# Thirty-two more empty columns in front of the split activations of a three-block transformer kernel

## Chip, core and metric

The kernel runs on one core of a Trainium2 chip. Its time is the device time of one execution in microseconds, of which the median over several executions counts; lower is better.

## What is computed

The reference chains three transformer blocks over one sequence of 512 tokens with 1024 channels, all in float32. Every dense layer is a product of the normed activations with a large weight matrix, and the feed-forward layers have an inner width of 2816.

```python
def reference(x, c, w_ada, ...):
    x = first_block(x, c, ...)     # ffn, spatial gating + forgetting attention, ffn
    x = second_block(x, ...)       # ffn, rwkv7 recurrence + convolution, ffn
    return third_block(x, ...)     # twice: sparse + differential attention, ffn

def swiglu(h, w_gate, w_up, w_down):
    return (jax.nn.silu(h @ w_gate) * (h @ w_up)) @ w_down
```

## The kernel before

The plan of the program (`whole_plan`) is a list of ten sublayers: six feed-forward layers (`ffn`) and four mixers. All large weight matrices are cut on the host into 264 units of 128 partitions by 2048 columns (1 MiB each). SyncE loads them one after the other into the two buffers of the tile `RAW` (`load`, L2093), each as soon as the unit two before it has been split.

A float32 product is computed as three products in the format fp32r. A unit is split by ScalarE into its rounded part (`WH`, L2435) and by VectorE into the rest (`WL = RAW - WH`, L2640). The activations are split in the same way: after a feed-forward boundary into `HH` and `HL`, after a mixer's boundary into `EH` and `EL` (`halves`), and the inner activations of a feed-forward layer into `AH` and `AL` (L2568, L2685). TensorE then multiplies high by high, high by low and low by high into the same PSUM bank; this is `mm3`, L2134 to L2138, and nearly all of TensorE's work goes through its three lines. Each of the matmuls is preceded by a load of its stationary operand.

`mm3` is used in two ways. In `project` (the first matmuls of a feed-forward layer and the projections of the mixers) a block of 128 columns of `WH` or `WL` is stationary, and 512 columns of `EH`, `EL`, `HH` or `HL` are moving. In `enter`, at the start of a sublayer, the same is done in halves of 256 columns, because the second half of the tokens arrives later. In `part` (the down projections, and the products that lead out of the mixers) the roles are turned: 128 tokens of `AH`, `AL`, `HH` or `HL` are stationary, and 512 columns of `WH` or `WL` are moving.

The tiles lie in SBUF in the order in which `build_program` asks for them, one behind the other, each rounded up to 32 bytes per partition. What comes ahead of the point that the change touches is, in bytes per partition, `X` (16384), `RAW`, `WH`, `WL` (16384 each), `A` (45056), `R`, `R0`, `V` (2048 each), `SG` (4096) and `ONES` (512): all multiples of 512. Then follow `PV` with 390 columns (1568 bytes after rounding), `CV` with 72 (288 bytes), `CN` with 776 (3104 bytes) and `LINE`, a tile of 8 columns (32 bytes) that nothing reads or writes. These four come to 4992 bytes, which is 9 times 512 and 384 more.

Behind `LINE` lie `E` (32768 bytes per partition), whose memory `EH` and `EL` share, and `G` (49152 bytes), whose memory `HH`, `HL`, `AH` and `AL` share, and then small tiles: `ST`, `ATT`, `IDB`, `MKC`, `MKB`, `PICK`, `FLOOR`, `W3`, `M8`, `GLU_LAST`, `LAM`, `PC2`. All split activations therefore start 384 bytes behind a multiple of 512 from the start of `X`, while `WH` and `WL` start on such a multiple.

The order of the work is set by the engines' own instruction streams and by semaphores; no address enters into it.

Of the kernel before, what the change touches and what calls it, by code (L numbers as in the profile page):

```python
# [25 lines left out]
P = 128  # L26
# [92 lines left out]
def build_program(nc, T, plan):  # L119
# [4 lines left out]
    def sb(name, shape, dt=F32):  # L124
        return ctx.enter_context(nc.sbuf_tensor(name, shape, dt))

    with ctx:
# [12 lines left out]
        PV = sb("PV", [P, T["pv"].shape[1]])  # L140
        CV = sb("CV", [P, VECTORS * KD])
        CN = sb("CN", [P, T["cn"].shape[1]])
        sb("LINE", [P, 8])
        with nc.sbuf_tensor("EH", [P, KD, S], F32R) as EH, nc.sbuf_tensor("EL", [P, KD, S], F32R) as EL:
            pass
        E = sb("E", [P, 16, S])
# [2956 lines left out]
def launch_parts(a, plan, nc):  # L3103
    arrays, cols, cncols = laid_out(a, plan)
    T = {n: nc.dram_tensor("in_" + n, x.shape, mybir.dt.from_np(x.dtype), kind="ExternalInput").ap()
         for n, x in arrays.items()}
    T["out"] = nc.dram_tensor("out_x", (S, D), F32, kind="ExternalOutput").ap()
    T["cols"], T["cncols"] = cols, cncols
    build_program(nc, T, plan)
    return {"in_" + n: x for n, x in arrays.items()}  # L3110
# [11 lines left out]
```

## Time and profile before

| | before |
|---|---|
| median of 3 runs | 3654.48 us (3650.88 to 3655.13) |
| the profiled execution | 3657.05 us |
| span of the profiled execution | 3655.3 us |
| TensorE matmul busy | 3482.2 us, 95% of the span, 19430 matmuls |
| weight loads busy | 2770.4 us, 76% |
| VectorE busy | 1837.7 us, 50% |
| ScalarE busy | 1152.5 us, 32% |
| GpSimd busy | 162.7 us, 4% |
| mean granted TensorE clock | 0.979 of 2.4 GHz |

In the names of instructions, `PS<-EH,WH` is a matmul into PSUM with `EH` as the moving and `WH` as the stationary operand; `128*128 128x512` means 128 partitions, 128 stationary columns and 512 moving columns. Both operands of a matmul of `mm3` are printed as f32. A matmul is shown from its start to the modelled end of its result, so that two neighbours overlap: what tells the pace is the distance from start to start. A window counts every instruction that overlaps it.

### The profile page before, as it was taken

How to read it: one execution, taken by the hardware profiler on the slowest of the kernel's cores; microseconds unless marked ns; L12 is line 12 of the kernel's file. 1: busy time of each engine (PE TensorE's matmuls, PEld its weight loads, DVE VectorE, ACT ScalarE, POOL GpSimd, SP SyncE). 2: the span in 40 equal slices, each digit the busy share in tenths (PEclk: the TensorE clock that was granted, in tenths of full speed). 3: DMA queues.
4: the chain of work that ended last, by engine and by line, in shares of the span. 5: the costliest groups of instructions: out<-in, count | busy, mean ns of one | idle time of the engine just before them, and what ended most of it. 6: DMA issues, size and time to landing. Idle time of an engine off the chain costs nothing.

```text
span 3655.3 us, 47516 instructions
## 1 busy us (share of the span) xinstructions
PE 3482.2 (95%) x19430; PEld 2770.4 (76%) x19436; DVE 1837.7 (50%) x2690; ACT 1152.5 (32%) x1728; POOL 162.7 (4%) x136
## 2 busy tenths in 40 slices
PE   9999899899999999998799999999999999899999
PEld 7887776678887888767588888666888886578887
DVE  6667535522334223798742225796422358952233
ACT  2222434422223222442342224335322233442222
POOL 0000000000000000000000001330000022200000
PEclk7999999999999999999999999999999999999999
DMA  6455221122222222220022222110222221112222
GB/s 245 178 182 196 81 95 47 58 81 92 92 92 88 100 94 92 81 79 15 8 87 92 96 98 94 70 69 24 81 93 100 95 93 70 47 53 92 92 93 81
DMA packets 47846, 330.29 MB, mean 90 GB/s; under 512 B 5312, under 2 KB 5568, under 8 KB 9280
## 3 DMA queue, kind: packets, MB, share of 16 engines
q1 hardware_dynamic: 41216, 290.09, 22.0%
q0 software_dynamic: 6464, 37.80, 2.8%
q8 instruction: 127, 2.08, 0.2%
q14 instruction: 39, 0.32, 0.0%
HBM read 325.77 MB, written 2.10 MB: 90 GB/s over the span
## 4 chain that ended last, share of the span: by engine, by line
PE 81%; DVE 13%; ACT 3%; issue 1%; DMA 0%; SPq 0%; DVEq 0%; ACTq 0%
PE PS L2136 24%; PE PS L2138 24%; PE PS L2137 24%; DVE WL L2640 2%; PE PS L319 1%; DVE A L1148 1%; DVE M L1147 1%; ACT WH L2435 1%; PE PS L394 1%; DVE X L2775 1%; PE PS L376 1%; PE PS L324 1%; PE PS L1493 1%; PE PS L931 1%; DVE A L2748 1%
## 5 line engine op out<-in xcount | busy, mean ns | idle before, releaser
L2640 DVE TENSOR_TENSOR WL<-RAW,WH 128x2048 fp32r<-128x2048 f32 x264 | 613.7, 2324 | 309.0 <-ACT WH L2435 308.6
L2136 PE MATMUL PS<-EH,WH 128*128 128x512 f32 (+1 forms) x1536 | 584.4, 380 | 28.9 <-DVE EL L2806 11.5
L2136 PE MATMUL PS<-HH,WH 128*128 128x512 f32 (+1 forms) x1456 | 556.0, 382 | 47.7 <-DVE HL L2806 23.4
L2137 PE MATMUL PS<-EL,WH 128*128 128x512 f32 (+1 forms) x1536 | 581.1, 378 | 0.0
L2138 PE MATMUL PS<-EH,WL 128*128 128x512 f32 (+1 forms) x1536 | 580.9, 378 | 0.0
L2435 ACT ACTIVATE WH<-RAW 128x2048 fp32r<-128x2048 f32 x264 | 503.9, 1909 | 191.6 <-PE PS L2138 183.5
L2137 PE MATMUL PS<-HL,WH 128*128 128x512 f32 (+1 forms) x1456 | 546.8, 376 | 0.0
L2138 PE MATMUL PS<-HH,WL 128*128 128x512 f32 (+1 forms) x1456 | 546.2, 375 | 0.0
L2679 DVE TENSOR_TENSOR A<-SG,PS 128x512 f32 (+1 forms) x132 | 90.7, 687 | 807.6 <-ACT SG L2565 807.6
L2565 ACT ACTIVATE SG<-PS 128x512 f32<-128x512 f32 x132 | 78.8, 597 | 1099.3 <-PE PS L2138 1099.3
L2136 PE MATMUL PS<-WH,AH 128*128 128x512 f32 x1056 | 417.7, 396 | 0.3 <-DVE CV L2868 0.3
L2138 PE MATMUL PS<-WH,AL 128*128 128x512 f32 x1056 | 417.1, 395 | 0.0
L2137 PE MATMUL PS<-WL,AH 128*128 128x512 f32 x1056 | 417.1, 395 | 0.0
L2136 PEld LDWEIGHTS PS<-HH,WH 128*128 128x128 f32 x1456 | 279.6, 192 | 114.6 <-issue 45.3
L2136 PEld LDWEIGHTS PS<-EH,WH 128*128 128x128 f32 x1536 | 291.8, 190 | 91.6 <-issue 13.6
L2138 PEld LDWEIGHTS PS<-EH,WL 128*128 128x128 f32 x1536 | 291.7, 190 | 58.6
L2137 PEld LDWEIGHTS PS<-EL,WH 128*128 128x128 f32 x1536 | 291.8, 190 | 58.4
L2138 PEld LDWEIGHTS PS<-HH,WL 128*128 128x128 f32 x1456 | 279.6, 192 | 52.2
L2137 PEld LDWEIGHTS PS<-HL,WH 128*128 128x128 f32 x1456 | 280.2, 192 | 50.5 <-issue 0.2
L2685 DVE TENSOR_TENSOR AL<-A,AH 128x1024 fp32r<-128x1024 f32 x66 | 80.3, 1224 | 368.6 <-ACT AH L2568 368.6
L2136 PEld LDWEIGHTS PS<-WH,AH 128*128 128x128 f32 x1056 | 198.4, 188 | 48.5 <-DVE CV L2868 0.4
L2138 PEld LDWEIGHTS PS<-WH,AL 128*128 128x128 f32 x1056 | 198.3, 188 | 47.8
(417 smaller groups left out, 3798.8 us busy)
## 6 DMA issues: line engine op xcount, KB each, us to landing
RAW<-in_w SPq DMA_DIRECT2D x264, 1024.0 KB, 4.8
E<-in_ada POOLq DMA_DIRECT2D x28, 1024.0 KB, 5.0
E<-in_ada SPq DMA_DIRECT2D x4, 1024.0 KB, 11.7
G<-in_ada SPq DMA_DIRECT2D x4, 1024.0 KB, 20.4
X<-in_x SPq DMA_DIRECT2D x1, 2048.0 KB, 13.9
X<-in_xn POOLq DMA_DIRECT2D x1, 2048.0 KB, 11.5
out_x<-A SPq DMA_DIRECT2D x4, 512.0 KB, 2.8
R<-in_row_ffn_post POOLq DMA_DIRECT2D x4, 256.0 KB, 3.1
```

Source lines behind the costliest of these rows:

```text
L319: nc.tensor.matmul(score_bank(x, i), pair["q"](i)[rows], pair["k"]((i + 1) * P)[rows], start=True, stop=False)
L324: last = nc.tensor.matmul(score_bank(x, i)[:, c0:c0 + right.shape[-1]], left, right, start=False, stop=a == len(added) - 1)
L376: last = nc.tensor.transpose(bank[:, c:c + P], probs(pair, g, x, i)[:, b * P:(b + 1) * P], IDENT)
L394: last = nc.tensor.matmul(PM[BANK_O][rows, b * P:S], pair["v"](x, b), PT[:, x, K_AT[b]:K_AT[b] + S - b * P], start=a == 0, stop=a == NT - 1)
L2136: nc.tensor.matmul(out, wh, xh, start=start, stop=False)
L2137: nc.tensor.matmul(out, wh, xl, start=False, stop=False)
L2138: return nc.tensor.matmul(out, wl, xh, start=False, stop=stop)
L2435: nc.scalar.activation(WH[:, w % 2, :], RAW[:, w % 2, :], ACT.Copy).then_inc(w_hi, 1)
L2565: nc.scalar.activation(SG[:, u % 2, :], PS[4 + 2 * (u % 2)][:], ACT.Silu).then_inc(silu_done, 1)
L2640: nc.vector.tensor_tensor(WL[:, w % 2, :], RAW[:, w % 2, :], WH[:, w % 2, :].bitcast(F32), ALU.subtract).then_inc(w_lo, 1)
L2679: nc.vector.tensor_tensor(A[:, bass.ds(u + i, 1), :].rearrange("p o s -> p (o s)"), SG[:, u % 2, :], PS[5 + 2 * (u % 2)][:], ALU.mult)\
L2685: nc.vector.tensor_tensor(AL[:, n % 2, :, :], A[:, bass.ds(2 * n + 2 * i, 2), :], AH[:, n % 2, :, :].bitcast(F32), ALU.subtract).then_inc( ...
```

## The change

The tile `LINE`, which holds no data, gets 40 columns instead of 8. Everything behind it in SBUF moves up by 128 bytes per partition: `E` with `EH` and `EL`, `G` with `HH`, `HL`, `AH` and `AL`, and the small tiles after them. The four tiles between `ONES` and `E` now come to 5120 bytes, ten times 512, so that the split activations start at a multiple of 512 bytes from `X`, as the split weights do. No instruction is added, removed or moved, and no wait changes.

```diff
@@ -140,7 +140,7 @@
         PV = sb("PV", [P, T["pv"].shape[1]])
         CV = sb("CV", [P, VECTORS * KD])
         CN = sb("CN", [P, T["cn"].shape[1]])
-        sb("LINE", [P, 8])
+        sb("LINE", [P, 40])
         with nc.sbuf_tensor("EH", [P, KD, S], F32R) as EH, nc.sbuf_tensor("EL", [P, KD, S], F32R) as EL:
             pass
         E = sb("E", [P, 16, S])
```

## Rows read from the trace of the kernel before

**Rows 1.** The page: busy times, TensorE's clock, and the chain that ended last.

```profile
PE 3482.2 (95%) x19430; PEld 2770.4 (76%) x19436; DVE 1837.7 (50%) x2690; ACT 1152.5 (32%) x1728; POOL 162.7 (4%) x136
...
PEclk7999999999999999999999999999999999999999
...
PE 81%; DVE 13%; ACT 3%; issue 1%; DMA 0%; SPq 0%; DVEq 0%; ACTq 0%
PE PS L2136 24%; PE PS L2138 24%; PE PS L2137 24%; DVE WL L2640 2%; PE PS L319 1%; DVE A L1148 1%; DVE M L1147 1%; ACT WH L2435 1%; PE PS L394 1%; DVE X L2775 1%; PE PS L376 1%; PE PS L324 1%; PE PS L1493 1%; PE PS L931 1%; DVE A L2748 1%
```

**Rows 2.** Groups of TensorE's matmuls by form: count, busy us, mean ns, idle before.

```profile
L2136 PE MATMUL PS<-EH,WH 128*128 128x512 f32 x1280 | 506.8, 396 | 6.8 <-DVE WL L2640 6.8
L2136 PE MATMUL PS<-HH,WH 128*128 128x512 f32 x1152 | 461.9, 401 | 11.9 <-DVE WL L2640 6.1 <-DVE HL L2658 2.9 <-DVE A L1848 1.9
L2136 PE MATMUL PS<-WH,AH 128*128 128x512 f32 x1056 | 417.7, 396 | 0.3 <-DVE CV L2868 0.3
L2136 PE MATMUL PS<-WH,HH 128*128 128x512 f32 x448 | 180.2, 402 | 9.1 <-DVE HL L2658 6.5 <-issue 1.7 <-DVE R L2651 0.9
L2136 PE MATMUL PS<-HH,WH 128*128 128x256 f32 x304 | 94.0, 309 | 35.8 <-DVE HL L2806 23.4 <-DVE HL L2803 12.5
L2136 PE MATMUL PS<-EH,WH 128*128 128x256 f32 x256 | 77.7, 303 | 22.2 <-DVE EL L2806 11.5 <-DVE EL L2803 10.7
```

**Rows 3.** Windows on TensorE: busy us (matmuls), granted clock, DMA share, GB/s.

```profile
760.00:960.00 200.00, 200.00 (x859) 1.00 0.25 89
990.00:1090.00 100.00, 100.00 (x430) 1.00 0.27 95
1140.00:1350.00 210.00, 210.00 (x901) 1.00 0.27 95
1390.00:1470.00 80.00, 80.00 (x345) 1.00 0.28 100
...
330.00:430.00 100.00, 100.00 (x432) 1.00 0.32 118
```

**Rows 4.** Timeline of 512-column matmuls with their weight loads: start, duration, instruction.

```profile
1000.23 0.40 PE L2138 MATMUL PS<-WH,AL 128*128 128x512 f32 x1
1000.23 0.19 PEld L2136 LDWEIGHTS PS<-WH,AH 128*128 128x128 f32 x1
1000.47 0.39 PE L2136 MATMUL PS<-WH,AH 128*128 128x512 f32 x1
1000.47 0.19 PEld L2137 LDWEIGHTS PS<-WL,AH 128*128 128x128 f32 x1
1000.70 0.40 PE L2137 MATMUL PS<-WL,AH 128*128 128x512 f32 x1
```

**Rows 5.** Timeline of 256-column matmuls on TensorE, 63 intervals between these two.

```profile
2969.71 0.28 PE L2138 MATMUL PS<-HH,WL 128*128 128x256 f32 x1
...
2977.19 0.28 PE L2138 MATMUL PS<-HH,WL 128*128 128x256 f32 x1
```

**Rows 6.** Groups of weight loads: 128 and 64 columns.

```profile
L2136 PEld LDWEIGHTS PS<-WH,AH 128*128 128x128 f32 x1056 | 198.4, 188 | 48.5 <-DVE CV L2868 0.4
...
L394 PEld LDWEIGHTS PS<-G,E 128*64 128x64 f32 x128 | 7.9, 136 | 11.2 <-issue 8.9 <-DVE A L509 1.9
```

**Rows 7.** Timeline of two sums over float32 tiles against `ONES`.

```profile
1767.72 3.70 PE L1630 MATMUL PS<-A,ONES 128*128 128x512 f32 x8
...
1778.76 3.70 PE L1640 MATMUL PS<-G,ONES 128*128 128x512 f32 x8 [1.14 <-ACT G L1773]
```

**Rows 8.** Groups of VectorE and ScalarE by form.

```profile
L2685 DVE TENSOR_TENSOR AL<-A,AH 128x1024 fp32r<-128x1024 f32 x66 | 80.3, 1224 | 368.6 <-ACT AH L2568 368.6
...
L1907 DVE TENSOR_TENSOR G<-G 128x512 f32<-128x512 f32 x12 | 8.2, 686 | 0.1
L1907 DVE TENSOR_TENSOR G<-A,G 128x512 f32<-128x512 f32 x12 | 8.2, 686 | 0.1
...
L2568 ACT ACTIVATE AH<-A 128x1024 fp32r x48 | 51.0, 1062 | 405.4 <-PE PS L2138 405.4
L2484 ACT ACTIVATE A<-X 128x1024 f32<-128x1024 f32 x40 | 42.5, 1064 | 82.3 <-DVE ST L2766 47.5 <-DVE X L2775 34.8
```

**Rows 9.** Groups within 900 to 950 us: the weights' split.

```profile
L2640 DVE TENSOR_TENSOR WL<-RAW,WH 128x2048 fp32r<-128x2048 f32 x5 | 11.5, 2293 | 5.1 <-ACT WH L2435 5.1
```

**Rows 10.** DMA issues: count, KB each, median us to landing.

```profile
RAW<-in_w SPq DMA_DIRECT2D x264, 1024.0 KB, 4.8
E<-in_ada POOLq DMA_DIRECT2D x28, 1024.0 KB, 5.0
```

## Prediction, made before the change was run

> **What bounds the kernel now.** I read the page first, for the shares and the chain that ended last. TensorE is busy for 95% of the span at a granted clock of nearly 1, and the chain runs over it for 81%, of which the three lines of `mm3` are 72% [rows 1]. So I went on to its matmuls by form. Each of `mm3`'s lines has the same counts: 1280 + 1152 + 1056 + 448 = 3936 matmuls of 512 columns, and 304 + 256 = 560 of 256 columns; three lines make 11808 and 1680 [rows 2]. Busy times overlap, so the pace has to come from windows without idle time and from the timeline. A window of 200 us in a feed-forward layer overlaps 859 matmuls; since each is drawn for 0.39 us and not 0.233, some 1.7 of them began before it, and 200 / 857.3 is 233.3 ns from start to start [rows 3]. The 256-column form takes (2977.19 - 2969.71) / 63 = 118.7 ns [rows 5]. In all 11808 x 0.2333 + 1680 x 0.1187 = 2755 + 199 = 2954 us, 81% of the span. The whole question is whether these two paces move; the instruction streams, waits and transfers are the same in both kernels. 1 ns on each 512-column matmul is 11.8 us, or 0.3% of the time.
>
> **Is there anything to win?** 512 columns at 2.4 GHz, the level that the granted clock of 1.00 stands for [rows 3], are 213.3 ns, and 256 are 106.7. The matmuls thus take 20.0 and 12.0 ns more than their columns. That excess, 11808 x 20.0 + 1680 x 12.0 = 256 us, is the most that any address could give back. The change can touch it only if it comes from where the operands lie. There are three ways, and the rows answer two.
>
> First, the place of the moving operand by itself. In the projections the moving operand is `EH` or `HH`, at 384 bytes past a multiple of 512, and the stationary one is `WH`, at 0. In the down products it is the other way round. The first sort stands in the windows from 760 and from 1140 us, the second in those from 990, 1390 and 330 us. By the same count, the paces are 233.3 and 233.5 ns for the first sort (200 / 857.3, 210 / 899.3), and 233.5, 233.0 and 232.4 ns for the second (100 / 428.3, 80 / 343.3, 100 / 430.3) [rows 3]. A matmul more or less at the edge of a window moves these by up to 0.7 ns, so they are one pace within 0.5%. A stream that begins at 0 is no faster than one that begins at 384, and so with the load. I book nothing for it.
>
> Second, the place of one operand against the other. Their distance modulo 512 is 384 or, with the roles turned, 128; the change makes it 0, which no fp32r matmul of this trace has. The nearest rows are float32 matmuls with the stationary `ONES`, at 0: eight with moving `A`, also at 0, and eight with moving `G`, at 384, take the same 3.70 us [rows 7]. They stream at about half the pace, so they speak for no effect but not at the full rate.
>
> Third, the overlap itself. The load of the next stationary block starts with the running matmul [rows 4]. A load of 128 columns takes 188 ns, one of 64 takes 136, so a column costs 0.81 ns and the reading of 128 some 104 ns, an estimate from these two [rows 6]. A 256-column matmul therefore has a load beside it nearly throughout; a 512-column one has the same single load and then 256 columns that run mostly alone. Those further 256 columns take 233.3 - 118.7 = 114.6 ns, against 106.7 by the clock: they are slow as well, by 7.9 ns. If clashes with the load made the excess, both widths would carry the same one, and they carry 12.0 and 20.0. Of each matmul's excess only 12.0 - 7.9 = 4.1 ns doesn't grow with the columns, and only that can be a clash with the load. Further, the load advances by 4 bytes in 0.81 ns and the stream by 4 bytes in about 0.42, so during one load the distance between their addresses runs through some 104 / 0.42 x 4 - 512 = 480 bytes, nearly a full turn of 512. Whatever clash there is at some distance is met in every load already; the start only shifts when. So I take 0 of the possible 4.1 ns, and keep 4.1 x (11808 + 1680) = 55 us either way as the bound.
>
> **The other engines.** `AL = A - AH` has operands at 0 and 384 and takes 1224 ns for 1024 columns; the weights' split has all its operands at 0 and takes 2293 for 2048 [rows 8, 9]. At 1069 ns for the further 1024 columns, both have a fixed part of 155 ns, so the distance costs nothing. `G<-G` and `G<-A,G` both take 686 ns [rows 8]. On ScalarE the same size takes 1062 ns from `A` into `AH` and 1064 from `X` into `A` [rows 8]. VectorE and ScalarE together have 16% of the chain [rows 1]; a 0.3% change there would be 1.8 us. Transfers of 1 MiB land after 5.0 us in `E` and 4.8 in `RAW` [rows 10], and they have no share in the chain [rows 1]. All of this I book at nothing; its bound is 2 us either way.
>
> **Sum.** 0 + 0 + 0: the profiled execution took 3657.05 us with a span of 3655.3; the median of the runs is 2.6 us below it, and I forecast the median unchanged, 3654 us.
>
> **A rule against it.** The trace shows 20.0 ns above the columns' time for every 512-column matmul and 12.0 for the 256-column ones [rows 3, 5]. The Trainium skill, page "TensorE: Matmul & The Clock Gate", section "Wait — 56ns, not 53.3ns?", gives a start-to-start distance of N / 2.4 GHz plus about 2.5 ns, so 215.8 ns at 512 columns; by it the sum would be (233.3 - 215.8) x 11808 + (118.7 - 109.2) x 1680, or about 223 us less, an estimate from that page. The trace doesn't agree with the rule for this format; if the address were the reason, it would.
>
> **Rivals.**
> - *The whole excess is an address effect.* Only the distance 0 lets a load and a stream share what they read, and everything above 213.3 and 106.7 ns can go, at most 256 us: 3398 us at the far end. Against it: the excess grows with columns that run beside no load, and turning the roles leaves it. For it: no row shows distance 0. Chance 0.04.
> - *The clash with the load goes, in part or whole.* This is the part of 4.1 ns: 55 us less at most, half of it as its likeliest size, 27 us, so 3627 us. For it: load and matmul start together in every pair [rows 4]. Against it: the full turn of the distance. Chance 0.13.
> - *Slower: at the same address the load and the stream begin in the same place.* They start together [rows 4], and with the distance 0 they ask for the same residue first. If the stream has to give way at its start, every matmul pays. A further 2.0 ns, half of the present fixed part, is 27 us: 3681 us. The far end is a pace that is at the longer of the two distances that the timeline shows in turn (0.24 and 0.23 us) [rows 4]: 0.0067 x 11808 = 79 us, 3733 us. It decides from 7.3 / 13488 = 0.54 ns per matmul on. Against it: a delayed load is hidden, for at 512 columns it ends 45 ns before the next matmul starts [rows 3, 6]. Chance 0.14.
> - *The change doesn't do what it says.* The sizes by tile give 1248 columns before and 1280 after, so `E` does move onto a multiple of 512 from `X`. Were it otherwise the time would be the same too; this is within the forecast.
>
> **How the numbers follow.** A measurement of this kernel can tell about 0.2%, 7.3 us, from no change: the three runs lie 4.3 us apart. Unchanged has 0.69. Faster has 0.04 + 0.13 = 0.17, slower 0.14. The unchanged case alone is 3647 to 3662 us. For 8 in 10 the range takes in the likeliest sizes of both smaller rivals, 3627 and 3681, with a little beyond them, as each is known only between 0 and its far end: 3615 to 3690 us. Left out are the large rival and the outer ends of the other two.
>
> **What would show it.** In the profile after, the window from 760 us should again overlap 858 to 860 matmuls in 200 us, and the 256-column matmuls stay at 118.7 ns. Groups of VectorE and ScalarE stay within a few ns. If the clash rival holds, both widths lose the same number of ns; if the whole excess is an address effect, the wide ones lose more; if it is slower, both gain equally, or the loads grow beyond 188 ns. What would make the forecast wrong is a special behaviour at distance 0 that neither 128 nor 384 shows.

## The result and the profile after

| | before | after |
|---|---|---|
| median | 3654.81 us | 3594.6 us |
| lowest and highest of 4 runs | 3650.88 to 3658.02 us | 3593.45 to 3597.33 us |
| span of the profiled execution | 3655.3 us | 3591.8 us |
| TensorE matmul busy | 3482.2 us | 3412.3 us |

The ratio is 0.9837 with a 95% interval of 0.982 to 0.9854: the kernel is 60 us faster, by 1.6%. The forecast was no change, with 3615 us as the low end of its range; the time lies below it.

The page after, its busy times and the chain, to be read against [rows 1]:

```profile
PE 3412.3 (95%) x19430; PEld 2768.7 (77%) x19436; DVE 1839.0 (51%) x2690; ACT 1153.0 (32%) x1728; POOL 160.8 (4%) x136
...
PE 81%; DVE 13%; ACT 4%; issue 1%; DMA 0%; SPq 0%; DVEq 0%; ACTq 0%
PE PS L2136 24%; PE PS L2138 24%; PE PS L2137 24%; DVE WL L2640 2%; PE PS L319 2%; DVE A L1148 1%; DVE M L1147 1%; ACT WH L2435 1%; PE PS L394 1%; DVE X L2775 1%; PE PS L376 1%; PE PS L324 1%; PE PS L931 1%; DVE A L2748 1%; PE PS L1493 1%
```

The counts are the same, and the shares within one point. Only TensorE's busy time has moved, by 69.9 us. Weight loads, VectorE and ScalarE stayed within 2 us. The windows on TensorE, against [rows 3] (busy us and matmuls, granted clock, DMA share, GB/s; the first two have the weights stationary, the last two the activations):

```profile
760.00:960.00 200.00, 200.00 (x884) 1.00 0.27 99
1140.00:1350.00 210.00, 210.00 (x928) 1.00 0.26 95
1385.00:1440.00 55.00, 55.00 (x243) 1.00 0.29 101
330.00:430.00 100.00, 100.00 (x446) 1.00 0.24 87
```

Where 859 matmuls overlapped 200 us there are now 884: 200 / 882.3 is 226.7 ns from start to start against 233.3, in either role, at the same granted clock. Over the whole trace, the mean of all distances of 512-column matmuls that follow without a gap is 226.9 ns after and 233.1 before. The 256-column ones went the other way. This is the stretch that answers [rows 5], with 76 intervals between the rows:

```profile
2914.74 0.28 PE L2137 MATMUL PS<-HL,WH 128*128 128x256 f32 x1
...
2923.86 0.28 PE L2138 MATMUL PS<-HH,WL 128*128 128x256 f32 x1
```

That is 120.0 ns against 118.7. The pairs of load and matmul look as before [rows 4], a load at the start of each matmul and 0.19 us long, only closer together:

```profile
810.32 0.39 PE L2136 MATMUL PS<-EH,WH 128*128 128x512 f32 x1
810.32 0.19 PEld L2137 LDWEIGHTS PS<-EL,WH 128*128 128x128 f32 x1
810.54 0.39 PE L2137 MATMUL PS<-EL,WH 128*128 128x512 f32 x1
```

The account closes within some 1 us: 11808 x 6.2 ns = 73 us less, 1680 x 1.0 ns (the mean over all 256-column matmuls) = 2 us more, 71 us together, against 69.9 us of busy time. TensorE's idle time, span less busy, rose from 173.1 to 179.5 us, so 6.4 us were given back. This rise is spread over many lines, none of them with more than some 2 us, and only part of it stands behind waits for ScalarE and VectorE, which did not become faster. 69.9 - 6.4 is the 63.5 us by which the span fell.

### The profile page after: what moved, and what is told of

The parts are those of the page before. It is cut to its first block, busy times and chain, and to the rows that moved or that the text cites. A ratio compares the mean times of both kernels' runs of the same rounds, so it can differ in the third digit from the quotient of the medians.

```text
span 3591.8 us, 47516 instructions
## 1 busy us (share of the span) xinstructions
PE 3412.3 (95%) x19430; PEld 2768.7 (77%) x19436; DVE 1839.0 (51%) x2690; ACT 1153.0 (32%) x1728; POOL 160.8 (4%) x136
## 4 chain that ended last, share of the span: by engine, by line
PE 81%; DVE 13%; ACT 4%; issue 1%; DMA 0%; SPq 0%; DVEq 0%; ACTq 0%
PE PS L2136 24%; PE PS L2138 24%; PE PS L2137 24%; DVE WL L2640 2%; PE PS L319 2%; DVE A L1148 1%; DVE M L1147 1%; ACT WH L2435 1%; PE PS L394 1%; DVE X L2775 1%; PE PS L376 1%; PE PS L324 1%; PE PS L931 1%; DVE A L2748 1%; PE PS L1493 1%
## 5 line engine op out<-in xcount | busy, mean ns | idle before, releaser
L2640 DVE TENSOR_TENSOR WL<-RAW,WH 128x2048 fp32r<-128x2048 f32 x264 | 614.6, 2328 | 303.0 <-ACT WH L2435 302.7
L2136 PE MATMUL PS<-EH,WH 128*128 128x512 f32 (+1 forms) x1536 | 577.1, 376 | 29.1 <-DVE EL L2806 11.3
L2137 PE MATMUL PS<-EL,WH 128*128 128x512 f32 (+1 forms) x1536 | 573.7, 374 | 0.0
L2138 PE MATMUL PS<-EH,WL 128*128 128x512 f32 (+1 forms) x1536 | 573.6, 373 | 0.0
L2685 DVE TENSOR_TENSOR AL<-A,AH 128x1024 fp32r<-128x1024 f32 x66 | 80.3, 1225 | 353.5 <-ACT AH L2568 353.5
```

The source lines that it names most:

```text
L2136: nc.tensor.matmul(out, wh, xh, start=start, stop=False)
L2137: nc.tensor.matmul(out, wh, xl, start=False, stop=False)
L2138: return nc.tensor.matmul(out, wl, xh, start=False, stop=stop)
L2640: nc.vector.tensor_tensor(WL[:, w % 2, :], RAW[:, w % 2, :], WH[:, w % 2, :].bitcast(F32), ALU.subtract).then_inc(w_lo, 1)
L2685: nc.vector.tensor_tensor(AL[:, n % 2, :, :], A[:, bass.ds(2 * n + 2 * i, 2), :], AH[:, n % 2, :, :].bitcast(F32), ALU.subtract).then_inc( ...
```

## Experiments

In all of them the *distance* is how far the stationary block starts behind the moving stream, in columns of 4 bytes.

### The distance over a whole turn

A kernel in which TensorE alone repeats one matmul 36 times for each of 85 settings:

```python
for n in range(N): last = mm(B[5][:, 0:512], W[:, 12:140], H[:, 0:512], start=n == 0, stop=n == N - 1)
```

> A kernel of its own that leaves out the whole computation and writes its input back: TensorE alone repeats one fp32r matmul 36 times per line, with the stationary block of 128 columns starting j columns (4 bytes each) behind a multiple of 512 bytes and the moving stream m0 columns behind one; then the same with other widths and formats. Distance theory (what counts is the place of the stationary block against the moving stream, modulo 512 bytes): 226.7 ns from start to start at j = 0, 233 ns at j = 32 (distance 384) and at j = 96 (distance 128), some curve between them, the same paces again at j = 128, 256, 512, and the pace of j = 0 at j = m0 = 32, 64 and 96. Alignment theory (what counts is that the activations' tiles start on a multiple of 512 bytes): moving streams at m0 = 0 all take 226.7 ns whatever j is, and those at m0 = 32 and 96 take 233. Theory that TensorE's pace only changes together with work of other engines: all lines take one pace, since no other engine works. For 256 columns: 120 ns at j = 0 and 119 at j = 32. No theory says anything of bf16 and float32; if the clash is one of reading 16-byte lines, bf16 should show about half the excess.

The timeline of this run; each row is one setting, and the start of the next row less its own, divided by 36, is the pace. L51 is distance 0, L52 is 4 columns, L53 is 8, and so on in steps of 4 to L82 with 124:

```profile
34.69 8.32 PE L51 MATMUL B<-H,W 128*128 128x512 f32 x36
42.85 8.33 PE L52 MATMUL B<-H,W 128*128 128x512 f32 x36
51.02 8.55 PE L53 MATMUL B<-H,W 128*128 128x512 f32 x36
59.41 8.56 PE L54 MATMUL B<-H,W 128*128 128x512 f32 x36
...
109.77 8.57 PE L60 MATMUL B<-H,W 128*128 128x512 f32 x36
...
134.84 8.40 PE L63 MATMUL B<-H,W 128*128 128x512 f32 x36
...
168.06 8.32 PE L67 MATMUL B<-H,W 128*128 128x512 f32 x36
176.22 8.33 PE L68 MATMUL B<-H,W 128*128 128x512 f32 x36
184.39 8.55 PE L69 MATMUL B<-H,W 128*128 128x512 f32 x36
...
384.22 8.33 PE L93 MATMUL B<-H,W 128*128 128x512 f32 x36
```

Distance 0 (L51) takes (42.85 - 34.69) / 36 = 226.7 ns, distance 8 (L53) 233.1, and distance 64 (L67) again 226.7. The curve repeats after 64 columns, 256 bytes: L67 to L69 are L51 to L53 once more. In steady state, as the mean over whole repeats of the pattern into which the distances from start to start fall, it reads as follows.

| distance modulo 64 columns | 0 | 4 | 8 to 16 | 20 | 24 | 28 to 40 | 44 | 48 | 52, 56 | 60 |
|---|---|---|---|---|---|---|---|---|---|---|
| ns per 512-column matmul | 226.7 | 226.7 | 233.3 | 232.0 | 234.3 | 233.3 | 230.0 | 228.9 | 233.3 | 226.7 |

The settings L83 to L88 have distances that are no multiple of 4 columns: 1, 2, 3, 5, 6 and 7 columns take 232.5, 230.6, 230.0, 233.3, 231.1 and 235.0 ns by the same subtraction. So an offset of a single column is enough to lose most of the gain.

Before, the distances were 32 modulo 64 in either role; after, 0. With both operands moved by 32, 96, 64 or 8 columns (L93 is the first) the pace is 226.7 ns: only the one against the other counts. A stream that starts on a multiple of 512 bytes is slow at most distances, so the alignment theory falls. No other engine worked, so the third theory falls as well. Also in this run: 256 columns take 120.0 ns at distance 0 and 118.8 at 32, 384 columns 173.3 and 176.0, 128 columns 111.7 at both. A bf16 matmul of 512 columns takes 215.8 ns and a float32 one two passes of 214.6 each on average (429.2), at every distance tried. Half the excess for bf16, which was expected if the clash is in reading 16 bytes at a time, did not show: it has 2.5 ns above its columns at each.

### Both operands off the multiple

```diff
+        sb("LINE_W", [P, 96])
         WH = sb("WH", [P, 2, UNIT], F32R)
...
-        sb("LINE", [P, 8])
+        sb("LINE", [P, 40])
```

> Split weights and split activations both start 384 bytes past a multiple of 512: an empty tile of 96 columns in front of WH, and LINE at 40 columns. Distance theory: the distance is 0 as in the changed kernel, so 512-column matmuls take 226.7 ns and the time is 3595 us, ratio 0.984. Alignment theory: activations off the multiple as before, so 233.3 ns and 3654 us, ratio 1.000.

3595.78 us against 3657.97, ratio 0.983 (0.9813 to 0.9846). The whole gain is there although neither weights nor activations start on a multiple of 512 bytes. The window of a projection has the count of the changed kernel:

```profile
760.00:960.00 200.00, 200.00 (x884) 1.00 0.27 95
```

### The activations 256 bytes off

```diff
-        sb("LINE", [P, 8])
+        sb("LINE", [P, 104])
```

> LINE at 104 columns: the activations start 256 bytes past a multiple of 512, the weights on one. Distance theory with a period of 512 bytes: neither the pace at 0 nor that at 128 or 384; with a period of 256 bytes: the same as at 0, 226.7 ns and 3595 us; with a period of 128 bytes the change could have done nothing. Alignment theory: 233.3 ns and 3654 us, as at 384.

3595.85 us, ratio 0.9834 (0.9817 to 0.985). The period of 256 bytes holds in the whole kernel; the 512 of the change is more than is needed.

### One part alone, and the other

```diff
+        sb("LINE_G", [P, 32])
         with nc.sbuf_tensor("HH", [P, KD, S], F32R) as HH, ...
```

> One part alone: LINE stays at 8 columns and an empty tile of 32 columns is put between E and G, so that HH, HL, AH and AL move to distance 0 while EH and EL stay at 384. Both theories: 226.7 ns in all 512-column matmuls with HH, HL, AH, AL (7968 of 11808), 233.3 ns in those with EH and EL; of the 60 us of the whole change about 40 us, so 3614 us, ratio 0.989. If the gain came from another tile behind E (the small ones), the paces would not follow the operands' names: all of it, or none.

3617.78 us, ratio 0.9895 (0.9879 to 0.9912), 40 us as expected. The counterpart, measured with a before of 3656.68 us:

```diff
-        sb("LINE", [P, 8])
+        sb("LINE", [P, 40])
...
+        sb("LINE_G", [P, 96])
         with nc.sbuf_tensor("HH", [P, KD, S], F32R) as HH, ...
```

> The other part alone: LINE at 40 columns and an empty tile of 96 columns between E and G, so that EH and EL are at distance 0 and HH, HL, AH, AL at 384 as before. Distance theory: 226.7 ns in the 3840 matmuls with EH and EL, 233 ns in the other 7968; the third of the gain that the run with G alone left, 20 us: ratio 0.9945. Together the two parts should give the 60 us of the whole.

3630.29 us, ratio 0.9926 (0.9909 to 0.9942): 26 us, somewhat more than the 20 expected. The two parts make 67 us, the whole 60 to 62; the intervals cover the difference. The pace follows the operands' names. Windows of the run with `G` alone, a stretch with `EH` and `EL`, then one with `HH` and `HL`:

```profile
760.00:960.00 200.00, 200.00 (x862) 1.00 0.26 94
1140.00:1340.00 200.00, 200.00 (x884) 1.00 0.28 97
```

And of the run with `E` alone:

```profile
760.00:960.00 200.00, 200.00 (x884) 1.00 0.26 95
1140.00:1340.00 200.00, 200.00 (x862) 1.00 0.26 93
```

884 is the fast pace. The 862 of the slow stretches is 232.5 ns, a little quicker than the 233.3 of the kernel before at the very same distance; the same pair of values, 232.4 and 233.3, stands in the windows of [rows 3]. It fits that the two parts add up to more than the whole: in each of these runs what stayed slow became 0.8 ns quicker.

### Distances that differ by role

```diff
-        sb("LINE", [P, 8])
+        sb("LINE", [P, 24])
```

> LINE at 24 columns: the activations start 448 bytes past a multiple of 512. From the sweep: where the weights are stationary (project, 7296 matmuls of 512 columns) the block lies 16 columns behind the stream modulo 64, 233.3 ns, unchanged; where the activations are stationary (part, 4512) it lies 48 columns behind, 228.9 ns. So 4512 x 4.4 = 20 us less: ratio 0.9945. The alignment theory, if anything were left of it: 1.000, and the same pace in both roles.

```diff
-        sb("LINE", [P, 8])
+        sb("LINE", [P, 56])
```

> LINE at 56 columns: the activations start 64 bytes past a multiple of 512, the mirror image. From the sweep: project at 48 columns, 228.9 ns, part at 16 columns, 233.3 ns. So 7296 x 4.4 = 32 us less: ratio 0.991, and the other role is the fast one.

Against 3656.68 us, the first took 3649.82 (0.9979, 0.9969 to 0.9989) and the second 3632.36 (0.9935, 0.9918 to 0.9951). The direction and the role are as the sweep has them, the sizes are smaller: 7 us instead of 20, and 24 instead of 32. The ten runs of the first lie between 3640.24 and 3651.34 us. In its profiled execution, which was the quickest of them, the matmuls of `part` took 227.5 to 231.7 ns, by their place in `mm3`, and those of `project` 233.3. The 256-column matmuls, whose stationary block now lies 16 columns behind the stream, changed as well. Here are two rows with 94 intervals between them:

```profile
2952.08 0.29 PE L2137 MATMUL PS<-HL,WH 128*128 128x256 f32 x1
...
2962.75 0.28 PE L2138 MATMUL PS<-HH,WL 128*128 128x256 f32 x1
```

That is 113.5 ns, against 118.7 before and 120.0 in the changed kernel. Of the kernels' 256-column paces the changed kernel has the slowest, and 1680 x 6.5 ns = 11 us lie between it and this one (an estimate from these rows). Windows of the run at 56 columns, `project` twice and then `part`:

```profile
760.00:960.00 200.00, 200.00 (x876) 1.00 0.27 95
1140.00:1340.00 200.00, 200.00 (x876) 1.00 0.27 95
1385.00:1435.00 50.00, 50.00 (x216) 1.00 0.26 91
```

876 are 228.8 ns, the 228.9 of the sweep. 216 in 50 us are 233.3.

### The width of the loaded block

> TensorE alone again, the computation left out: the stationary block is 128, 96, 64 or 32 columns wide. At 226.7 ns an fp32r matmul is still 32 cycles of 2.4 GHz above its 512 columns. Clash theory (each 16-byte line of the block that is loaded beside the matmul costs the stream one cycle where load and stream meet well, and more where they meet badly): at distance 0 the excess follows the width of the block, 32, 24, 16 and 8 cycles, so 226.7, 223.3, 220.0 and 216.7 ns; at distance 32 columns also less for narrower blocks, 233.3 falling to some 218. Rival (the excess belongs to the fp32r stream itself, and the load only shifts it): 226.7 ns at every width. A moving operand that stays on one column reads no new lines: by the clash theory near 215.8 ns at every distance. The three matmuls of mm3 in turn give the same paces as one repeated, 226.7 and 233.3 ns.

A kernel like the first, with `W[:, j:j + w]` as the stationary block. Its timeline, with the same subtraction over 36: blocks of 64 columns at the distances 0, 8 and 24 (L61 to L63), blocks of 32 columns at 8 (L67), then a moving operand that stays on one column (L75, L76) and a stationary one that does (L77, L78), each at the distances 0 and 32:

```profile
117.21 8.44 PE L61 MATMUL B<-H,W 128*64 128x512 f32 x36
125.49 8.50 PE L62 MATMUL B<-H,W 128*64 128x512 f32 x36
133.82 8.32 PE L63 MATMUL B<-H,W 128*64 128x512 f32 x36
141.99 8.42 PE L64 MATMUL B<-H,W 128*64 128x512 f32 x36
...
166.81 8.75 PE L67 MATMUL B<-H,W 128*32 128x512 f32 x36
175.40 8.46 PE L68 MATMUL B<-H,W 128*32 128x512 f32 x36
...
216.81 8.03 PE L75 MATMUL B<-H,W 128*128 128x512 f32 x36
224.68 8.03 PE L76 MATMUL B<-H,W 128*128 128x512 f32 x36
232.55 8.50 PE L77 MATMUL B<-H,W 128*128 128x512 f32 x36
240.89 8.50 PE L78 MATMUL B<-H,W 128*128 128x512 f32 x36
249.23 8.56 PE L79 MATMUL B<-H,W 128*128 128x512 f32 x36
```

With 512 moving columns at distance 0, blocks of 128, 96, 64 and 32 columns take 226.7, 230.0, 230.0 and 231.7 ns. Neither theory holds: the excess doesn't fall with the block, and it isn't constant. Nor is distance 0 the best one for a narrow block: 64 columns take 226.7 ns at distance 24 (L63), and 32 columns at distance 8 settle at 240.0 ns (L67), the slowest pace of all.

With a moving operand that stays on one column the pace is 218.7 ns at both distances, so more than half of the excess hangs on the stream's reading of new columns. With a stationary operand that stays on one column it is 231.7 ns at both distances. So the distance stops counting when either operand stands still. The three matmuls of `mm3` in turn give 226.7 ns at distance 0 and 232.4 at 32.

And three distances did not repeat. 4 columns gave 233.3 ns where the first sweep had 226.7, 60 columns 228.3 against 226.7, and 32 columns 232.4 against 233.3. In the first sweep 4 columns ran behind distance 0, which is fast, but 60 ran behind 56, which is slow. With the stream moved instead of the block, the distances of 4 and 60 columns gave further values, 236.8 ns for 4 columns (in this run) and 231.6 for 60 (in the first).

### What came before

> TensorE alone, the computation left out. Each of ten distances runs 200 times three times over, behind a lead-in of 36 matmuls at j = 0, at j = 24, and with a block of 32 columns. Locking theory (load and stream fall into a rhythm that depends on how they came in, and keep it): j = 0 and 64 take 226.7 ns behind every lead-in, j = 8, 16, 24, 32 and 40 some 233, but j = 4, 48 and 60, which differed or stood between in the two sweeps, differ by their lead-in, with values from 226.7 to 233.4. Rival (the pace belongs to the distance alone, and the sweeps differed by chance): each distance shows one value. Then blocks of 1, 4, 16, 32, 64 and 128 columns, 100 times each, against 512 and 256 moving columns: if part of the excess is the stream's own, a block of 1 column still leaves 226.7 ns and 113.3 ns, 1/16 above the columns; if all of it is the load's, 216 and 109 ns.

The timeline of this run, 200 matmuls each; the same subtraction, divided by 200. Distance 0 behind the three lead-ins (L51, L53, L55), then 4 columns (L57, L59, L61), then 60 columns (L63, L65, L67):

```profile
88.15 45.52 PE L53 MATMUL B<-H,W 128*128 128x512 f32 x200
133.51 8.50 PE L54 MATMUL B<-H,W 128*32 128x512 f32 x36
...
195.38 45.50 PE L57 MATMUL B<-H,W 128*128 128x512 f32 x200
240.72 8.59 PE L58 MATMUL B<-H,W 128*128 128x512 f32 x36
249.15 46.83 PE L59 MATMUL B<-H,W 128*128 128x512 f32 x200
295.81 8.49 PE L60 MATMUL B<-H,W 128*32 128x512 f32 x36
...
359.00 45.50 PE L63 MATMUL B<-H,W 128*128 128x512 f32 x200
404.34 8.60 PE L64 MATMUL B<-H,W 128*128 128x512 f32 x36
412.77 45.83 PE L65 MATMUL B<-H,W 128*128 128x512 f32 x200
458.44 8.50 PE L66 MATMUL B<-H,W 128*32 128x512 f32 x36
```

Four columns take (240.72 - 195.38) / 200 = 226.7 ns behind a lead-in at distance 0, and (295.81 - 249.15) / 200 = 233.3 behind one at 24, and they keep it for all 200. Sixty columns take 226.7 or 228.3. Distance 0, and 64 likewise, comes back to 226.7 behind every lead-in: L53, behind distance 24, is at (133.51 - 88.15) / 200 = 226.8 with its first few included. The distances 8, 16, 24, 32, 40 and 48 showed one value each, 233.3, 233.3, 234.3, 232.4, 233.3 and 228.9. So the locking theory holds for 4 and 60 columns, 16 bytes to either side of a multiple of 256. It holds for 32 columns over the runs taken together: in the first sweep, behind 28 columns, the starts lay 229 and 238 ns apart in turn, 233.3 in the mean, while here and in the run before they repeat after seven matmuls, at 232.4. These are the two values that the whole kernels show at this distance. Of the distances tried, only the multiples of 64 columns are fast whatever came before.

Blocks of 1 column take 228.9 ns against 512 moving columns and 116.7 against 256; the last four rows of the timeline are blocks of 64 and 128 columns:

```profile
1798.81 11.52 PE L118 MATMUL B<-H,W 128*64 128x256 f32 x100
1810.16 23.16 PE L119 MATMUL B<-H,W 128*64 128x512 f32 x100
1833.15 12.16 PE L120 MATMUL B<-H,W 128*128 128x256 f32 x100
1845.15 22.86 PE L121 MATMUL B<-H,W 128*128 128x512 f32 x100
```

A block of 64 columns takes 113.5 ns against 256 moving columns, 128 columns take 120.0. With a load of a single column, which still takes 82 ns against 188, the excess is 15.6 ns at 512 columns. So most of it is probably the fp32r stream's own; a stream without loads would have to show it.

### One line off the changed kernel

```diff
-        sb("LINE", [P, 8])
+        sb("LINE", [P, 44])
```

> LINE at 44 columns: the activations start 16 bytes past a multiple of 512, one 16-byte line off the changed kernel. The first sweep gave 226.7 ns at one line either way, the second 233.4 and 228.3. If the first holds in the whole kernel: 3595 us, ratio 0.983. If the second holds: project at j = 60 takes 228.3 ns and part at j = 4 takes 233.4, so 7296 x 5 = 36 us less than before, ratio 0.990. The locking theory allows either, and runs of the same kernel may differ from each other by more than 4 us.

3658.08 us against 3654.93, ratio 1.0011 (1.0001 to 1.002). Neither forecast came true; the whole gain is gone:

```profile
760.00:960.00 200.00, 200.00 (x859) 1.00 0.25 89
1140.00:1340.00 200.00, 200.00 (x859) 1.00 0.27 95
1385.00:1435.00 50.00, 50.00 (x216) 1.00 0.27 92
```

All three are at 233.3 ns. For `part` (4 columns) that is the slow one of its two rhythms; for `project` (60 columns) it is a value beside the 226.7, 228.3 and 231.6 that TensorE alone showed. Sixteen bytes of an empty tile took back the whole gain.

## Why the prediction was wrong

**What held.** The step that reduced the question to two paces was right: instruction streams, transfers, VectorE and ScalarE are unchanged, within 2 us, and the counts of [rows 2] times the change of pace give the 69.9 us of busy time within some 1 us. So was the place of an operand by itself: runs with both operands shifted are as fast as with both on the multiple. And most of the excess above the columns' time does stay at the best distance: 226.7 - 213.3 = 13.3 ns of 20.0. A block of one column leaves 15.6 ns, so it is probably the stream's own, as the step on the further 256 columns had it.

**The step that failed** is the third, the overlap of load and stream, in both its halves.

The first half was the split of the excess. I held that a clash with the load costs both widths the same, so that only 12.0 - 7.9 = 4.1 ns could be one. The runs show that what hangs on the distance is not the same at each width: going from distance 32 to 0, 512 columns gain 6.7 ns, 384 gain 2.7, 128 nothing, and 256 *lose* 1.2. I take from the repeating patterns of starts that load and stream fall into a rhythm, of which the length of the matmul is a part. The term was booked at 0 and bounded at 4.1 ns per matmul; in the kernel it measured 6.2 on the 512-column form, with the opposite sign on the other.

The second half was the full turn: as the distance runs through 480 bytes during a load, every clash would be met wherever it starts. The sweep shows a curve from 226.7 to 235.0 ns, so the start doesn't drop out, although the true turn is 256 bytes and a load runs through nearly two of them. The argument takes both as running at fixed paces. The last runs speak against it: at 4 columns one and the same pair of addresses has two paces, and keeps the one it came in with. I read this as each clash shifting the next, of which an average over a turn says nothing.

**The rivals.** The clash rival was right by place, the block against the stream, and mis-sized: its far end, 55 us, was 5 us short of the result, its likeliest size 27. Its own mark, that both widths lose the same, was wrong. For the rival of the whole excess, the wide ones lost more as it said, but 13.3 ns stayed. The slower rival, a clash at the start of each pair, was not seen at distance 0 at all for 512 columns. The 256-column matmuls did become slower, by 1.2 ns, but no run shows that their start is the reason. The rule of the Trainium skill, page "TensorE: Matmul & The Clock Gate", section "Wait — 56ns, not 53.3ns?" (215.8 ns at 512 columns), agrees with the bf16 matmuls here, 215.8 ns at every distance tried, and not with fp32r, 226.7 at best.

**The range.** The prediction itself said that no fp32r matmul of the trace had distance 0, and that the nearest rows, [rows 7], stream at half the pace. They were no witness: the sweep has float32 at 429.2 ns at every distance tried. And the two distances that it did have, 384 and 128 bytes, are one and the same modulo 256: their equal paces, which the prediction held against an effect of the address ("turning the roles leaves it"), were one point measured twice. So a distance that no row showed was booked at 0.

**A reading that said nothing.** The step on the other engines took one fixed part of 155 ns from two VectorE durations. Any two durations have one, so this showed nothing of the distance. The booking at nothing was right all the same: the same two groups have 1225 and 2328 ns after and 1224 and 2324 before, over the whole run.

**What stays open.** What in SBUF makes 256 bytes the period, and why 60 columns gave 233.3 ns in the whole kernel, was not settled. That load and stream meet in the reading is inferred: the distance between them is what counts, and as soon as one of them stays on one column there is no dependence. A stream with no load at all was not tried.

## What to carry to other kernels

Where a kernel's time is fp32r matmuls of 512 moving columns on blocks of 128, place the stationary and the moving tiles so that their distance is a multiple of 256 bytes; here that was 2.9% of the pace and 1.6% of the time, for nothing. Leave no smaller offset: 16 bytes gave the gain away, and a rhythm that is quick in one run can be slow in the next. For other widths measure anew: 256 moving columns were quickest at 64 bytes, and a block of 64 columns at 96. The size of an empty tile is then part of the tuning, and any tile that changes its width ahead of it has to be made up for.

Before two equal measurements are taken as proof that a distance doesn't matter, ask by which period they could be the same point.

## What the runs showed of the hardware

- An fp32r matmul of 512 columns on a block of 128 takes 226.7 ns at best at the 2.4 GHz level, 13.3 ns above its columns, and up to 235.0 in the sweep by the distance of its operands modulo 256 bytes (236.8 in one setting at 16 bytes); bf16 takes 215.8 and float32 429.2 at any distance tried.
- The same distance can have two steady paces: 226.7 and 233.3 ns at 16 bytes to one side of a multiple, 226.7 and 228.3 to the other, 233.3 and 232.4 at 128 bytes. At 16 bytes the matmuls ahead decide which.
- When either operand stays on one column, the distance no longer counts: 218.7 ns with the moving one, 231.7 with the stationary one, at 0 and at 128 bytes.
- At 256 columns the best distance for 512 is the slowest of those seen, 120.0 ns against 118.7 at 128 bytes and 113.5 at 64; the kernel at distance 0 pays this 1680 times, some 2 us against the kernel before.
